# Identity turns on TensorE behind the barrier of every dense stage and ahead of the first expert work

## The reference, cut to what matters

```
for layer in range(2):
    x = x + hybrid_mixer(rmsnorm(x), ...)          # proj, delta rule, attention, pooling, w_out
    x = x + (swiglu(rmsnorm(x)) if layer == 0 else moe_swiglu(rmsnorm(x)))   # 8 experts, top 2
x = x + mix(rms_norm(x))                           # proj, RWKV-7 and RG-LRU branches, gates, out
x = x + cross_attention(rms_norm(x), rms_norm(mem))
x = x + conv_ffn(rms_norm(x))
return rms_norm(x)
```

## Time and profile before

| | |
|---|---|
| median of 3 runs | 2937.83 us (2930.48 to 2938.72) |
| the profiled execution's own time | 2927.05 us |
| its span, first to last instruction | 2925.3 us |
| around the span | 1.75 us |
| TensorE matmul busy | 2702.9 us (92% of the span), 22883 instructions |
| DVE, ACT, POOL busy | 54%, 41%, 11% |
| mean granted TensorE clock | 0.961 of full |
| DMA | 332.30 MB, mean 114 GB/s |

### The profile page before, as it was taken

The page is one execution under the profiler, slowest core; times in us unless marked ns, Lnnn a source line. Parts: engine busy times, 40 slices in busy tenths (PEclk is TensorE's granted clock), DMA queues, the critical chain, the costliest instruction groups (busy, mean ns, idle before and its releaser), DMA issues. The chain is left out here.

```text
span 2925.3 us, 54871 instructions
## 1 busy us (share of the span) xinstructions
PE 2702.9 (92%) x22883; PEld 2112.8 (72%) x22883; DVE 1576.0 (54%) x1934; ACT 1193.2 (41%) x1517; POOL 320.8 (11%) x356
## 2 busy tenths in 40 slices
PE   8999899999999987999999998987789999999998
PEld 6676678888767665777787776843677777778887
DVE  6647354343664655656666666356635544454453
ACT  5544242122454434555555554244314433433232
POOL 5022000000202210111001111022210000000002
PEclk9999899999999997999999998998989999999999
DMA  4200234233320015777777776311004331434232
GB/s 134 71 9 3 58 108 117 77 91 85 98 65 9 3 51 196 250 249 250 265 239 246 255 251 220 87 44 50 7 3 130 94 108 65 111 84 120 74 103 62
DMA packets 351955, 332.30 MB, mean 114 GB/s; under 512 B 17273, under 2 KB 269525, under 8 KB 351605
## 3 DMA queue, kind: packets, MB, share of 16 engines
q1 hardware_dynamic: 348101, 317.76, 35.0%
q0 software_dynamic: 3392, 11.14, 1.1%
q10 hardware_dynamic: 240, 0.07, 0.0%
HBM read 317.41 MB, written 11.53 MB: 112 GB/s over the span
## 5 line engine op out<-in xcount | busy, mean ns | idle before, releaser
L2913 DVE TENSOR_TENSOR experts_w_lo<-experts_raw,experts_w_hi 128x2048 fp32r<-128x2048 f32 (+1 forms) x162 | 336.0, 2080 | 225.1 <-ACT experts_w_hi L2870 210.2
L2870 ACT ACTIVATE experts_w_hi<-experts_raw 128x2048 fp32r<-128x2048 f32 (+1 forms) x162 | 282.1, 1749 | 225.0 <-DMA experts_raw<-in_moe_down 92.1
L3069 PE MATMUL experts_psum<-experts_w_hi,experts_xg_lo 128*128 128x512 f32 x384 | 162.8, 424 | 30.8 <-DVE experts_w_lo L2913 16.5
L1380 PE MATMUL proj_psum<-keep_act_hi,proj_w_lo 128*128 128x512 f32 x384 | 164.5, 428 | 15.1 <-DVE keep_act_lo L290 11.2
L3071 PE MATMUL experts_psum<-experts_w_hi,experts_xg_hi 128*128 128x512 f32 x384 | 157.1, 409 | 0.0
L3070 PE MATMUL experts_psum<-experts_w_lo,experts_xg_hi 128*128 128x512 f32 x384 | 156.7, 408 | 0.0
L1382 PE MATMUL proj_psum<-keep_act_hi,proj_w_hi 128*128 128x512 f32 x384 | 155.1, 404 | 0.0
L1381 PE MATMUL proj_psum<-keep_act_lo,proj_w_hi 128*128 128x512 f32 x384 | 154.7, 403 | 0.0
L689 PE MATMUL conv_ffn_psum<-keep_act_hi,conv_ffn_w_lo 128*128 128x512 f32 x352 | 140.6, 400 | 5.0 <-DVE keep_act_lo L290 4.9
L689 PE MATMUL ffn_psum<-keep_act_hi,ffn_w_lo 128*128 128x512 f32 x352 | 140.5, 399 | 4.9 <-DVE keep_act_lo L290 4.9
L691 PE MATMUL conv_ffn_psum<-keep_act_hi,conv_ffn_w_hi 128*128 128x512 f32 x352 | 139.9, 397 | 0.0
(11 more groups left out here) (789 smaller groups left out, 6581.7 us busy)
## 6 DMA issues: line engine op xcount, KB each, us to landing
experts_raw<-in_moe_gate SPq DMA_DIRECT2D x50, 1024.0 KB, 6.4
experts_raw<-in_moe_up SPq DMA_DIRECT2D x48, 1024.0 KB, 7.1
experts_raw<-in_moe_down SPq DMA_DIRECT2D x64, 768.0 KB, 6.1
conv_ffn_raw<-in_w_ffn_in SPq DMA_DIRECT2D x43, 512.0 KB, 4.9
proj_raw<-in_w_in SPq DMA_DIRECT2D x18, 768.0 KB, 4.3
ffn_raw<-in_ffn_up SPq DMA_DIRECT2D x22, 512.0 KB, 5.2
ffn_raw<-in_ffn_down SPq DMA_DIRECT2D x16, 704.0 KB, 5.6
conv_ffn_raw<-in_w_ffn_out SPq DMA_DIRECT2D x16, 704.0 KB, 5.7
```

The source lines that it names most:

```text
L1380: pe.matmul(out, lo, m.act_hi[:, x, :], start=x == 0, stop=False)
L2870: act.activation(w_hi[v % 2][:, s], raw[ring][:, 0:n], ACT.Copy).then_inc(rounded, 1)
L2913: dve.tensor_tensor(w_lo[v % 2][:, s], raw[(2 * v + q) % RING][:, 0:n], w_hi[v % 2][:, s].bitcast(F32), ALU.subtract).then_inc(split, 1)
L3069: pe.matmul(out, lhs[1][:, first + k, :], w_hi[slot][:, cols], start=begin and k == 0, stop=False)
```

## The change

A helper turns the identity into a PSUM region n times (out = identity transposed; nobody reads it, and the next real matmul into that bank starts a new sum). Nothing is removed or moved.

```diff
+def turn_identity(m, pe, out, n):
+
+    for _ in range(n):
+        pe.transpose(out, m.ident[:, :], m.ident[:, :])

 # dense_phase, tensor stream
             pe.nop().then_inc(full, 2)
+            if first:
+                turn_identity(m, pe, ps[:, bank(0, 0), 0:P], 18)
             for j, job in enumerate(jobs):

 # woven_phase, tensor stream
         def _(pe):
+            turn_identity(m, pe, ps[:, bank(0), 0:P], 18)
             for h, (g, k) in enumerate(halves):

 # experts_phase, tensor stream
             pe.nop().then_inc(silu_done, 1)
+            turn_identity(m, pe, ps[:, 7, 0:P], 10)
             list_slots(0)
+            turn_identity(m, pe, ps[:, 7, 0:P], 54)
             turn_rows(0)
```

## The result

The changed kernel takes 2957.47 us (median of four runs, 2954.44 to 2963.2) against 2936.3 for the kernel before on the same chip: ratio 1.0077, 95% interval 1.0055 to 1.0099. It is 21 us slower. I had forecast 2929.5 us and a range that ended at 2939.

A forecast was written before the change was run, and what follows sets the result against it. TensorE, busy 92% of the span, was taken as the bound, slowed by half clock at nine starts. Starts -7.5, merge +0.3 and experts +0.7 made -6.5 us, -7.5 for a typical run: 2929.5 us, range 2919 to 2939.

The forecast's parts named there:

- The nine starts: Starts of nine dense stages: first matmuls run at half clock for 38.32 us in all; turns gain 9.0, allowed 7.5 us.
- The new wait behind the second weights: In ffn, proj2, cross_proj and conv_ffn: TensorE at full clock waits 1.2 us for DVE's split of the second group's weights.
- the bound I had written: At the two w_outs: turns run at half clock are 1.2 us too long for the idle time.
- Turns bring the clock up: At the dense starts: transposes alone raise the clock to full, as 32 transposes behind the experts did in the trace.
- The 0.6 us by which I had them too long: In ffn, proj2, cross_proj, w_co and conv_ffn: 18 turns at half clock outlast the idle time by 0.6 us.
- Merge +0.3: In merge: 18 turns push a side job by 2.0 us, but late x tiles leave +0.3 us, 2.0 at most.
- Experts +0.7: Expert phase: ten turns start the first list 0.9 us late, delaying the second unit; +0.7 us, ends 0.2 and 1.2.
- the sum itself: -7.5 + 0.3 + 0.7: Whole kernel: dense starts, merge and experts give -6.5 us in the profiled execution, -7.5 us for a typical run.
- The rivals: Whole kernel: gain swallowed, 2935 to 2936 (chance 0.20); longer stretches saved, 2926 (0.15); turns never lift the clock, 2949 (0.06).
- Turns never lift the clock: Whole kernel: turns and the matmuls behind them stay at half clock; +11.6 us with merge, 2949 us, chance 0.06.
- What would show it wrong: Windows at 0.50 during and behind turns, first matmuls over 3.4 us after the barrier, or row transposes starting behind turns.

The follow-up runs named there:

- with the loop held in place: Changed kernel without expert turns, 8 and 68 empty instructions (nops) instead, loop one whole block further on than in the kernel before: 2923.91 us, ratio 0.9966.
- The two kernels with the longer body: Changed kernel with 62 expert turns in place of 54, plus 60 or 100 nops ending each loop item: 85.3 to 85.5 or 95.3 to 95.8 us an item.
- single runs with empty instructions alone: Kernel before plus only nops counting up an unawaited semaphore, ahead of the expert loop: 2971.67 us with 52, 2899.63 us with 68.

## Why the prediction was wrong

- **The nine starts.** Gain 9.0 us, allowed down to 7.5. Measured: 8.3 us over the ten phases in the profiles (merge, at +0.1, included), and a ratio of 0.9966 with the loop held in place. It stands in every profile: these ten phases take 1621.7 to 1625.1 us in the seven kernels with turns at the starts and 1631.3 to 1633.0 us in the five without. Stage by stage: proj layer 1 -2.6 and w_co -1.5 (predicted 1.1 and 1.5); proj2 -1.2, conv_ffn -0.9, ffn -0.2 and cross_proj -0.2 (1.4, 0.7, 0.3, 0.3); w_out -0.6 twice (1.2 and 0.8); proj layer 0 -0.6 (1.7). **The total came out right, in part by luck.** Only 1.05 us of the 2.6 of proj layer 1 lie at its start, as predicted (by its 60th matmul). The other 1.5 come 142 us behind the barrier, where the kernel before falls to half once more for 3.4 us, and so do all five kernels without turns at the starts and none of the seven with them (rows below, before and after). I had no term for that, and why it goes is open. Without it the nine starts gave 6.8 us, not 9.0; proj layer 0 and the w_outs fell short. The new wait behind the second weights is there, 1.03 us on L639 in ffn where I had 1.2. In w_out the turns ran at half and made the first matmul 1.0 us late (3.79 and 3.68 us behind the barrier against 2.72), the bound I had written. Proj layer 0 stayed partly at half (0.61).

```profile
885.60:888.90 3.30, 3.30 (x10) 0.50 0.01 2
```

```profile
883.10:886.40 3.30, 3.30 (x12) 1.00 0.01 2
```

```profile
383.86 0.47 PE L697 MATMUL ffn_psum<-keep_act_hi,ffn_w_lo 128*128 128x512 f32 x1 [1.03 <-DVE ffn_w_lo L639]
```

- **Turns bring the clock up: right at the two w_outs; at most starts they did something else.** In w_out the turns began at half and the clock came up in their row. But in ffn, proj layer 1, cross_proj, w_co and conv_ffn nothing had to be brought up. The clock had not fallen yet when the turns began, 1.2 to 1.8 us behind TensorE's last work, they ran at full themselves (18 in 2.15 us, not 3.8), and it never fell; so in all seven kernels with turns. Without them TensorE idles 4.3 us or more there, and in all five kernels without turns the clock falls. The 0.6 us by which I had them too long at these starts did not arise. Turns in w_out and in ffn, in the changed kernel:

```profile
317.84:321.17 3.33, 3.33 (x16) 0.50 0.64 182
```

```profile
368.16:370.31 2.15, 2.15 (x18) 1.00 0.38 103
```

The rule of the Trainium skill that I had priced against it ("TensorE: Matmul & The Clock Gate", Part 4: transpose mode doesn't count as busy) doesn't hold for these: at w_out the clock rose behind 3.3 us of turns alone, and at the other starts it stayed up with them and fell without.

- **Merge +0.3:** measured +0.1.

- **Experts +0.7, by the first list and rows: right as far as it went.** The first list starts 2.87 us behind the barrier instead of 1.95 (0.9 late, as written). The second unit starts 26.1 us behind it instead of 25.1, and the first item is 0.7 us longer. The 54 turns were mis-sized: I had 5.9 us; they took 8.3 and pushed the row transposes, because the clock was at half for the first half of them. It cost next to nothing.

```profile
1116.38 2.37 PE L44 MATMUL experts_psum<-keep_ident 128*128 128x128 f32 x10 [2.06 <-PEq L67]
1118.54 1.71 PE L3012 MATMUL experts_psum<-moe_lists,experts_pick 128*128 128x3 f32 x8
...
1121.81 8.48 PE L44 MATMUL experts_psum<-keep_ident 128*128 128x128 f32 x54
1130.13 1.04 PE L3021 MATMUL experts_psum<-keep_ident,experts_xg 128*128 128x128 f32 x8
```

- **The step that failed is the sum itself: -7.5 + 0.3 + 0.7.** It prices turns by the time that they run and has no term for where they push what follows: the experts' +0.7 covers the first item alone, and every further pass is put at nothing, without a reason. The 308 instructions ahead of the loop over the items moved it from a place with one stall at each jump (3.7 to 5.3 us) to one with two (4.2 to 4.9 and 3.4 to 4.2 us). The second stall comes because the loop starts just ahead of a block's end: seven instructions in, TensorE needs the next block. That gave +33.7 us where I had +0.7: 26.7 us are the seven second stalls, 2 us the longer first ones, 0.7 us the first item; the other 4 us or so are not split up (the clock over the phase was 0.94 against 0.95). Chunk gave +5.8 where I had nothing; its cause is open (below).

- **The rivals.** None of them was this. "Turns never lift the clock" ended on the slower side, at 2949, by a mechanism that did not happen (its parts add up to 11.3, not 11.6). Of the three signs in "What would show it wrong", two did show, in small: the first matmuls of both w_outs came later than 3.4 us behind the barrier, and the row transposes started behind the turns and not behind the DMA. They cost 1.0 us each and next to nothing. The clock, the sign on which most hung, came out right, and none of the three pointed at the loop.

- **What was to be seen.** The rows were in the profile before: the earlier trace rows stop at the first item, and I never laid a window at the second. There stood 3.66 us of "issue" in front of a loop start, and in the page 184 packets on a queue called instruction. Neither says which way 308 instructions would push. But a cost of some 5 us at seven jumps, whose size hangs on a place, would have been a rival worth 35 us to either side, and no forecast of 7 us is safe beside that.

Whether the body stays in the engine hangs on how many blocks it touches, as the runs show: a body over seven blocks stays (0 packets at seven jumps), over eight it is fetched whole (63 packets, nine an item). The Trainium skill ("Advanced Engine Details and Errata", ISA Cache) states lines of 16 KB or 256 instructions, and 128 KB for TensorE; divided, that is an estimate of eight lines. The runs agree with the line (packets of 16384 bytes, a period of 256). The same section says "Only 2 cache lines!", and that doesn't hold for TensorE here, since seven blocks stay. An eighth line for the block behind the body would explain why seven is the limit and why nine come; that last point is argued, not shown.

**Left open.** Chunk, 3072 small matmuls in a straight line, takes a q8 packet each 3.8 us (24 in 92.08 us). Over ten kernels its time followed its own place: 92.1 us at 0 past a block, 93.6 at 36, 95.4 at 52, 97.7 at 68, 97.9 at 88, 99.3 at 104, 100.7 at 128, 94.4 at 160, 92.1 and 91.3 at 216. (The two kernels with the longer body, 94.3 and 93.6, don't stand in this row, since their body moves chunk too.) A straight line has no jump, so the cause is another; how fetches and the small matmuls' own waits meet there wasn't tried. The attention cores differ from run to run (127.6 to 131.3 us in five kernels whose code up to them is that of the kernel before, 124.8 to 131.9 in the seven with turns at the starts). That is scatter, and it makes up much of what single runs differ by.

## What to carry to other kernels

An instruction that costs nothing where it stands still moves everything behind it on its engine. If an engine's loop has a body near the size that the engine can keep, read the first rows behind each jump back and the packets of its instruction queue, and place the loop (a few nops in an idle stretch ahead of it) before measuring anything else. When a small edit shows a change of a per cent in a loop that it doesn't touch, hold the loop's place with padding and measure the edit again: here the edit is worth -0.3%, the place +1.2% or -1.3% (single runs with empty instructions alone).

## What the runs showed of the hardware

- TensorE's instructions arrive in packets of 16384 bytes, 256 instructions. A body of 1717 instructions over seven blocks is read once; over eight, all of it comes again in each pass, with a stall at the jump of 3.4 to 6.1 us, and a second of 3.4 to 4.2 us if a block ends seven instructions behind the loop's start. The stalls end 1.3 to 1.9 us behind the landing of a packet (kernel before and changed kernel). Between the two extremes lie 72 us of 2900, by sixteen empty instructions.
- The clock is lower where the stalls are: over the expert phase it was 0.94 with two stalls, 0.95 with one, 0.99 with none, and the first matmul of a triple took 425, 424 and 410 ns in the mean.
- A clock that is still up is kept by work in the gap. With 18 turns begun 1.2 to 1.8 us behind the last work it stayed at 1.00 at five starts in seven kernels; with TensorE idle for 4.3 us or more it fell at the same starts in five kernels.
- An empty instruction took TensorE's sequencer 0.15 us; 112 of them, at two places where TensorE waits, were not free: the four phases around them grew by 7.5 us.
- The profile puts the same stall down to "issue" at one jump and to a DVE wait at the next (three and four of the seven in the kernel before). A wait that goes when nothing is changed but the place was never the wait that it was named for.
